# A hybrid decoder trunk on one Trainium2 core: the first layer's input projection in another order of column chunks

## The chip, the cores and the metric

The kernel runs on one core of a Trainium2 chip. The metric is the device time of one execution in microseconds (us), lower is better. A core has TensorE (PE, with its weight loads shown as PEld), VectorE (DVE), ScalarE (ACT), GpSimd (POOL) and SyncE (SP, which here issues nearly all plain DMAs), and 16 DMA engines that serve them.

## The reference

Two residual layers over 512 rows of 1024 float32 values. What matters here is the first half of layer 0:

```python
xn = rms_norm(x, mix_norm_even[i])
proj = jnp.einsum('bsd,de->bse', xn, w_in[i])
au, av, q, kc, vc, ks, vs, kw, vw, gl = jnp.split(proj, split_points, axis=-1)
ya = chunked_spatial_gating(au, av, ...)                  # gelu(au) * (W_s @ rms_norm(gelu(av)) + b_s)
yb = native_sparse_attention(q, kc, vc, ks, vs, kw, vw, gl, ...)
x = x + jnp.einsum('bse,ed->bsd', jnp.concatenate([ya, yb], axis=-1), w_out[i])
# inside the attention: 8 query heads, 2 kv heads, head size 64
q = rms_norm(q.reshape(bsz, seq, G, H, D), q_gain) * (HEAD_DIM ** -0.5)
k_cmp = rms_norm(compress(kc, w_cmp_k), k_gain[0]); v_cmp = compress(vc, w_cmp_v)
ks, kw = rms_norm(ks, k_gain[1]), rms_norm(kw, k_gain[2])
g = jax.nn.sigmoid(gate_logits)                           # weights of the three branches
```

The 2328 columns of `w_in` are: au 512, av 512, q 512, six tensors of 128 (kc, vc, ks, vs, kw, vw) and 24 gate logits. After this half comes a mixture of 32 experts (its weights are most of the bytes), and then layer 1: a pooling mixer and a second mixture of experts. All is float32.

## The kernel before

It is written engine by engine, each with its own instruction stream in program order; semaphores join them. The 512 rows are four blocks of 128 (`NB = 4`), the 1024 inputs are eight blocks (`KD = 8`).

**Projection.** `x_transpose(b)` transposes a row block on PE into banks 0 to 3, ACT and DVE copy it out with the norm's gain (`x_out`), and ACT and DVE make its root mean square (`square`, `mean`, `root`, `rroot`). The projection goes by column chunks, in the order of the list `CH`: q (512 columns), kc to vs (512), kw, vw and gates (280), a_v (512), a_u (512). `project(ch, b)` is one tile: eight products of 128 x 128 by 128 x n into bank 4 + i % 4, with i = 4 ch + b. From i = 4 on it waits until the tile four places back has been copied out (`s_pe_`). `proj_tile(ch, b)` is ACT's copy of that tile to SBUF, scaled by the row's 1/rms; a_v goes through Gelu and is squared there.

**Weights of the chunks.** There are two buffers, `win[0]` and `win[1]`; chunk ch goes to `win[ch % 2]`. SP issues, in its program order: the first row block of x, the first gain, chunk 0 (in two halves, L457), the other three row blocks, chunk 1, 14 small loads and the router's, the weights of the first expert pair (`load_gate_up(0, 0, ...)` L431, `load_down` L442), zeros for a DRAM buffer (L486), and only then chunk 2, when chunk 0 has been multiplied (`s_pj`, L422). Behind it come the four loads of the compression weights (L496), chunk 3 when chunk 1 is done, and chunk 4 when chunk 2 is done. All of these are on one hardware DMA queue.

```python
for ch in range(2, len(CH)):
    sp.wait_ge(s_pj, 4 * (ch - 1))
    load_win(ch)
```

**Head norms.** When all of the first three chunks are copied out, ACT squares q, ks and kw (L842, L844, L845), DVE sums them by head (L1146 to L1148), ACT takes the root (L847), DVE inverts it (L1153) and scales q in four instructions and the keys in eight (L1077 under `tt`). Behind that in DVE's program stand the inputs of the compression: copies of the transposed kc and vc (L1169) and additions into `cmp_in`. PE meanwhile transposes kc and vc (L1618), runs `project(3, 0)` and `project(3, 1)`, waits for the scaled q and keys (`s_qk_n` 6), transposes three blocks of q, and waits for `s_ci` before the 256 small products of the compression (L1652). `project(3, 2)`, more transposes, `project(3, 3)` and the a_u tiles (`gate_rows`, L1674) follow, these between the 32 attention units.

**Gates.** ACT makes exp(-rstd * logit) straight from the product's bank, from `minus_rstd` that DVE prepares (L1141).

Of the kernel before, what the change touches and what calls it, by code (L numbers as in the profile page):

```python
# [20 lines left out]
ALU = mybir.AluOpType  # L21
# [3 lines left out]
P = 128  # L25
# [20 lines left out]
def build(nc, t):  # L46
    ctx = ExitStack()
    with ctx:
# [3 lines left out]
        def sem(name):  # L52
            return ctx.enter_context(nc.semaphore(name))
# [48 lines left out]
        vrstd = mix[:, 528:544]  # L102
        minus_rstd = vrstd[:, 0:NB]
        gate = mix[:, 544:640]
# [17 lines left out]
        def bank(i):  # L122
# [63 lines left out]

        CH = [("q", 1024, 512), ("kc_vc_ks_vs", 1536, 512), ("kw_vw_gates", 2048, 280),
              ("a_v", 512, 512), ("a_u", 0, 512)]
# [12 lines left out]
        s_w = sems("win_loaded", len(CH))  # L201
        s_w0b = sem("first_win_second_half_loaded")
        s_gain = sem("first_gain_loaded")
# [198 lines left out]
        def _(sp):  # L402
# [50 lines left out]

            w_first = t["w_in"][0].rearrange("(p k) n -> p k n", k=KD)
            for h in range(2):
                ks = slice(4 * h, 4 * h + 4)
                sp.dma_start(win[0].rearrange("p (k n) -> p k n", k=KD)[:, ks, :],  # L457
                             w_first[:, ks, CH[0][1]:CH[0][1] + 512]).then_inc(s_w0b if h else s_w[0], 16)
            for b in range(1, NB):
# [288 lines left out]
        def _(act):  # L748
# [20 lines left out]
            def rows(n, b):  # L769
                act.wait_ge(s_rs, stat(n, b) + 1)  # L770
                if n == 3 and b < NB - 1:
                    act.wait_ge(s_pt2, b + 2)
                if n == 3:
                    act.wait_ge(s_pt2, b + 1)
                a.activation(xs[:, b, :], x3[:, b, :], ACT.Copy,
                             scale=rstd[:, n * NB + b:n * NB + b + 1]).then_inc(s_xs[b], 1)
# [39 lines left out]
            def proj_tile(ch, b):  # L816
                i = 4 * ch + b
                act.wait_ge(s_pj, i + 1)
                src = bank(4 + i % 4)
                own = rstd[:, b:b + 1]  # L820
                if ch == 0:
                    act.wait_ge(s_rs, stat(0, b))

                    a.activation(q[:, b, :].rearrange("p (i g d) -> p g i d", i=4, g=2),
                                 src.rearrange("p (g i d) -> p g i d", g=2, i=4), ACT.Copy, scale=own).then_inc(s_pe_, 1)
                elif ch == 1:
                    a.activation(kv[:, b, 0:512], src, ACT.Copy, scale=own).then_inc(s_pe_, 1)
                elif ch == 2:
                    act.wait_ge(s_rs, stat(0, NB - 1) + 1)
                    a.activation(kv[:, b, 512:768], src[:, 0:256], ACT.Copy, scale=own)  # L830
                    a.activation(gate[:, b * 24:(b + 1) * 24], src[:, 256:280], ACT.Exp,
                                 scale=minus_rstd[:, b:b + 1]).then_inc(s_pe_, 1)
                else:
                    a.activation(v[:, b, :], src, ACT.Gelu, scale=own).then_inc(s_pe_, 1)
                    act.wait_ge(s_pe_, i + 1)
                    a.activation(v_squares[:, b, :], v[:, b, :], ACT.Square).then_inc(s_vs, 1)

            for ch in range(3):
                for b in range(NB):
                    proj_tile(ch, b)  # L840
            act.wait_ge(s_pe_, 12)
            a.activation(squares.rearrange("p (b c) -> p b c", b=NB), q, ACT.Square).then_inc(s_hs, 1)  # L842
            sq2 = squares2.rearrange("p (r b c) -> p r b c", r=2, b=NB)
            a.activation(sq2[:, 0], kv[:, :, 256:384], ACT.Square).then_inc(s_hs, 1)  # L844
            a.activation(sq2[:, 1], kv[:, :, 512:640], ACT.Square).then_inc(s_hs, 1)  # L845
            act.wait_ge(s_mean, 1)
            a.activation(hstd[:, :], hsq[:, :], ACT.Sqrt).then_inc(s_std, 1)  # L847
            act.wait_ge(s_small, SMALL)
            link(a.activation(q_gain[:, :], q_gain[:, :], ACT.Copy, scale=HD ** -0.5))

            def q_out(i):
                act.wait_ge(s_mt, 3 + i)
                a.activation(qT[:, i, :], bank((0, 1, 3, 0)[i]), ACT.Copy, scale=q_gain[:, 0:1]).then_inc(s_mta, 1)
# [9 lines left out]
            proj_tile(3, 0)  # L863
            proj_tile(3, 1)
            act.wait_ge(s_cm, 1)
            q_out(0)
            q_out(1)
            q_out(2)
            act.wait_ge(s_mean, 2)
            a.activation(csq[0:HD, 1:2], csq[0:HD, 0:1], ACT.Sqrt).then_inc(s_std, 1)  # L870
            proj_tile(3, 2)
            q_out(3)
            k_out(0)
            k_out(1)
            proj_tile(3, 3)
            act.wait_ge(s_mean, 3)
            a.activation(vstd[:, :], vsq[:, :], ACT.Sqrt).then_inc(s_std, 1)
# [189 lines left out]
        def _(dve):  # L1067
# [71 lines left out]
            rroot(0, NB - 1)  # L1139
            dve.wait_ge(s_rs, stat(0, NB - 1))  # L1140
            ve.tensor_scalar(minus_rstd, rstd[:, 0:NB], -1.0, None, ALU.mult).then_inc(s_rs, 1)  # L1141
            dve.wait_ge(s_small, SMALL)


            dve.wait_ge(s_hs, 3)
            ve.tensor_reduce(hsq[:, 0:32], squares.rearrange("p (a d) -> p a d", d=HD), AX, ALU.add)  # L1146
            link(ve.tensor_reduce(hsq[:, 32:48], squares2.rearrange("p (a d) -> p a d", d=HD), AX, ALU.add))
            ve.tensor_scalar(hsq[:, :], hsq[:, :], 1.0 / HD, EPS, ALU.mult, ALU.add).then_inc(s_mean, 1)  # L1148

            link(ve.tensor_scalar(gate[:, :], gate[:, :], 1.0, None, ALU.add))  # L1150
            ve.reciprocal(gate[:, :], gate[:, :])
            dve.wait_ge(s_std, 1)
            link(ve.reciprocal(hrstd[:, :], hstd[:, :]))  # L1153
            qv = q.rearrange("p b (h d) -> p b h d", d=HD)
            hv = hrstd[:, 0:32].rearrange("p (b h) -> p b h", b=NB)
            for b in range(NB):
                tt(qv[:, b], qv[:, b], bc(hv[:, b], 2, [P, NH, HD]), ALU.mult).then_inc(s_qk_n, 1)
            for r in range(2):
                c0 = 256 + 256 * r
# [5 lines left out]

            dve.wait_ge(s_cz, 2)
            for r in range(2):
                dve.wait_ge(s_mt, 1 + r)
                link(ve.tensor_copy(rawT[:, r, :], bank(r)))  # L1169
                dve.sem_inc(s_mtv, 1)  # L1170
                for half in range(2):
# [15 lines left out]
            v_sum(0)  # L1187
            v_sum(1)

# [10 lines left out]
            ins.then_inc(s_vb, 1)  # L1200
            dve.wait_ge(s_std, 2)
            link(ve.reciprocal(csq[0:HD, 2:3], csq[0:HD, 1:2]))
            link(ve.tensor_scalar(kcn[0:HD, 0:HD], kcn[0:HD, 0:HD], csq[0:HD, 2:3], None, ALU.mult))
            link(tt(kcn[0:HD, 0:HD], kcn[0:HD, 0:HD], kc_gain[0:HD, :], ALU.mult))
            ve.tensor_copy(kcn[0:HD, HD:2 * HD], kcn[0:HD, 0:HD]).then_inc(s_kn, 1)
            v_sum(2)
            dve.wait_ge(s_kt, 1)
# [80 lines left out]
            maxes(1)  # L1288
            dve.wait_ge(s_std, 3)
            ve.reciprocal(vrstd[:, :], vstd[:, :]).then_inc(s_vn, 1)  # L1290
# [47 lines left out]
            def route(l):  # L1338
                lgt = rt["lgt"].rearrange("p (b c) -> p b c", b=NB)
                n = 1 + 2 * l  # L1340
                dve.wait_ge(s_lg, NB * (l + 1))
                dve.wait_ge(s_rs, stat(n, NB - 1) + 1)
                link(tt(lgt, bank(LOGIT_BANK[l])[:, 0:144].rearrange("p (b c) -> p b c", b=NB),
# [211 lines left out]
        def _(pe_):  # L1555
# [41 lines left out]
            def project(ch, b):  # L1597
# [10 lines left out]
                for k in range(KD):  # L1608
                    if i == 0 and k == 4:
                        pe_.wait_ge(s_w0b, 16)  # L1610
                    ins = mm(bank(4 + i % 4)[:, 0:n], xT[:, k, b * P:(b + 1) * P], w[:, k, :],  # L1611
                             start=(k == 0), stop=(k == KD - 1))
# [16 lines left out]
            for ch in range(1, 3):  # L1629
                for b in range(NB):  # L1630
                    project(ch, b)

            pe_.wait_ge(s_pe_, 8)
            transpose_blocks(bank(0), kv, 0)
            transpose_blocks(bank(1), kv, P)
            project(3, 0)
            project(3, 1)
            pe_.wait_ge(s_qk_n, 6)
            pe_.wait_ge(s_mtv, 1)
            transpose_blocks(bank(0), q, 0)  # L1640
            pe_.wait_ge(s_mtv, 2)
            transpose_blocks(bank(1), q, P)
            transpose_blocks(bank(3), q, 2 * P)

# [420 lines left out]
```

## Time and profile before

| | before |
|---|---|
| Median of 3 runs | 896.33 us (894.91, 896.59, 896.33) |
| The profiled execution's own time | 892.19 us |
| Its span in the trace | 890.4 us |
| PE busy | 791.5 us, 89% of the span |
| ACT, DVE busy | 242.6 us, 255.4 us |
| Projection, chunks 0 to 2, in the trace | 9.9 to 85.3 us |
| Chunk 3 with compression and transposes | 85.3 to 124.9 us |
| First attention units on | from 128.5 us |

The span is what the hardware profiler recorded between the first and last instruction; the profiled execution's own time has 1.8 us around it. A timeline line gives start, duration, engine, line of the program, and in square brackets the idle time before it and who ended it. "DMA to landing" counts from the start of the issuing instruction on SP to the moment the data are announced.

### The profile page before, as it was taken

The page shows a single profiled execution, that of the slowest core. Times are in us where ns is not written, and L with a number is a line of the kernel's source. Part 1 is how long each engine was busy: PE and PEld are TensorE (multiplying, and loading weights), DVE is VectorE, ACT ScalarE, POOL GpSimd, SP SyncE. Part 2 cuts the span into 40 slices and gives each one's busy share as a digit, 9 for nine tenths or more (in the row PEclk, how much of TensorE's full clock was granted, in tenths as well). Part 3 has the DMA queues.
Part 4 walks back from the last instruction along what each step waited for, and adds up shares of the span by engine and source line. Part 5 has one row for each costly group of instructions (what it writes and reads, how often), then busy time and mean ns, then how long its engine had stood idle before and what let it go on. Part 6 is the DMA issues. An engine that isn't in the chain of part 4 may idle for free.

```text
span 890.4 us, 10328 instructions
## 1 busy us (share of the span) xinstructions
PE 791.5 (89%) x3981; PEld 375.3 (42%) x3981; DVE 255.4 (29%) x577; ACT 242.6 (27%) x584; POOL 100.1 (11%) x164
## 2 busy tenths in 40 slices
PE   6999899999999989998877978899999996797965
PEld 3447444555555633333322322397433332332321
DVE  0100727566462351111101111554511111111106
ACT  3303355554344411221101111364012211111111
POOL 2000000000002510111101001130111111011000
PEclk9999999999999999999988999999999999888998
DMA  8898130200002599999999999996399999999986
GB/s 287 259 328 189 64 78 18 95 2 1 0 1 79 205 404 406 416 357 421 421 421 419 419 415 391 386 421 252 141 392 418 419 419 423 420 420 418 406 312 253
DMA packets 74912, 258.09 MB, mean 290 GB/s; under 512 B 28017, under 2 KB 29553, under 8 KB 54896
## 3 DMA queue, kind: packets, MB, share of 16 engines
q1 hardware_dynamic: 65936, 241.16, 69.2%
q0 software_dynamic: 8928, 16.27, 4.9%
q8 instruction: 32, 0.52, 0.2%
q14 instruction: 16, 0.13, 0.0%
HBM read 247.44 MB, written 26.21 MB: 307 GB/s over the span
## 4 chain that ended last, share of the span: by engine, by line
PE 71%; DMA 10%; DVE 8%; issue 4%; ACT 3%; SPq 3%; DVEq 1%; POOLq 0%
PE ps L1884 22%; PE ps L1898 10%; PE ps L1611 10%; PE ps L1762 6%; DMA rest<-in_w_exp_down_dram 5%; PE ps L1878 3%; PE ps L1674 3%; PE ps L1818 2%; PE ps L1573 2%; PE ps L1686 2%; PE ps L1830 2%; SPq L442 2%; DMA norm<-expert_rows 2%; PE ps L2013 2%; PE ps L1591 2%
## 5 line engine op out<-in xcount | busy, mean ns | idle before, releaser
L1884 PE MATMUL ps<-w_pair,tmp 128*64 128x512 f32 x704 | 172.1, 644 | 38.1 <-issue 17.7
L1884 PEld LDWEIGHTS ps<-w_pair,tmp 128*64 128x64 f32 x704 | 55.8, 148 | 140.2 <-issue 124.9
L1611 PE MATMUL ps<-w_pair,norm 128*128 128x512 f32 (+1 forms) x256 | 100.5, 552 | 4.2 <-DMA w_pair<-in_w_in_dram 3.7
L1077 DVE TENSOR_TENSOR tmp<-tmp,ps 128x256 f32<-128x256 f32 (+1 forms) x34 | 13.8, 407 | 294.7 <-ACT tmp L962 294.7
L962 ACT ACTIVATE tmp<-ps 128x256 f32<-128x256 f32 x32 | 12.3, 384 | 272.4 <-PE ps L1884 272.4
L1898 PE MATMUL ps<-w_pair,tmp 128*64 128x512 f32 x352 | 80.4, 598 | 3.2 <-ACT tmp L965 2.0
L1884 PE MATMUL ps<-norm,tmp 128*64 128x512 f32 x320 | 72.8, 607 | 10.5 <-issue 7.3
L1611 PEld LDWEIGHTS ps<-w_pair,norm 128*128 128x128 f32 x256 | 48.8, 193 | 52.3 <-issue 45.2
L657 POOL DMA_INDIRECT expert_rows<-tmp x30 | 30.2, 1005 | 331.1 <-DVE tmp L1467 314.2
L1762 PE MATMUL ps<-w_pair,norm 128*128 128x512 f32 x128 | 58.0, 593 | 0.0
L957 ACT ACTIVATE tmp<-ps,gains 128x128 f32<-128x128 f32 x128 | 36.6, 369 | 61.1 <-PE ps L1878 61.1
L1467 DVE COPY tmp<-ps 128x512 f32<-128x512 f32 x30 | 20.8, 692 | 93.3 <-PE ps L1898 93.3
L651 POOL DMA_INDIRECT tmp<-norm_rows,tmp x32 | 32.8, 1026 | 119.2 <-DVEq L1424 57.6
L1884 PEld LDWEIGHTS ps<-norm,tmp 128*64 128x64 f32 x320 | 23.6, 139 | 52.5 <-issue 47.2
L1878 PEld LDWEIGHTS ps<-ident,tmp 128*128 128x128 f32 x256 | 31.1, 194 | 32.3 <-issue 29.5
L1573 PE MATMUL ps<-masks 128*128 128x512 bf16 x186 | 44.7, 400 | 0.0
L1878 PE MATMUL ps<-ident,tmp 128*128 128x128 f32 x256 | 36.8, 287 | 7.4 <-issue 6.9
L1898 PEld LDWEIGHTS ps<-w_pair,tmp 128*64 128x64 f32 x352 | 23.7, 136 | 43.5 <-issue 38.8
L973 ACT ACTIVATE tmp<-ps 128x512 f32<-128x512 f32 x30 | 17.9, 598 | 82.6 <-PE ps L1898 82.6
L921 ACT ACTIVATE rest<-ps 128x768 f32<-128x768 f32 (+3 forms) x32 | 21.6, 677 | 64.0 <-PE ps L1818 64.0
L1898 PE MATMUL ps<-rest,tmp 128*64 128x512 f32 x160 | 36.5, 597 | 2.5 <-DMA rest<-in_w_exp_down_dram 2.5
L889 ACT ACTIVATE rest<-ps,mix_small 128x384 f32<-128x384 f32 (+3 forms) x64 | 32.3, 511 | 3.4 <-DVE mix_small L1271 3.1
(241 smaller groups left out, 832.7 us busy)
## 6 DMA issues: line engine op xcount, KB each, us to landing
w_pair<-in_w_exp_gate_dram SPq DMA_DIRECT2D x44, 1024.0 KB, 17.6
w_pair<-in_w_exp_up_dram SPq DMA_DIRECT2D x44, 1024.0 KB, 26.1
w_pair<-in_w_exp_down_dram SPq DMA_DIRECT2D x40, 1024.0 KB, 26.9
rest<-in_w_exp_down_dram SPq DMA_DIRECT2D x20, 1024.0 KB, 22.1
norm<-in_w_exp_gate_dram SPq DMA_DIRECT2D x20, 1024.0 KB, 23.1
norm<-in_w_exp_up_dram SPq DMA_DIRECT2D x20, 1024.0 KB, 27.6
norm<-expert_rows SPq DMA_DIRECT2D x16, 512.0 KB, 8.3
w_pair<-in_w_in_dram SPq DMA_DIRECT2D x3, 2048.0 KB, 10.1
```

What stands on the lines that cost most here:

```text
L651: return pool.indirect_dma_start(out=buf, out_offset=None, in_=norm_dram, in_offset=bass.IndirectOffsetOnAxis(ap=index, axis=0), bounds_ch ...
L657: return pool.indirect_dma_start(out=out_dram, out_offset=bass.IndirectOffsetOnAxis(ap=index, axis=0), in_=buf, in_offset=None, bounds_che ...
L889: ins = a.activation(prob[:, n % 2, h, 0:width], bank(2 * (n % 2) + h)[:, 0:width], ACT.Exp, bias=nmax[:, 2 * n + h:2 * n + h + 1], accum_ ...
L921: a.activation(pT[:, n % 2, 0:nb], ps[2][:, :, :].rearrange("p c n -> p (c n)")[:, 0:256 * nb] .rearrange("p (a h t) -> p a h t", h=2, t=P ...
L957: ins = a.activation(xgT[:, k, :], bank(0)[:, k * P:(k + 1) * P], ACT.Copy, scale=gain_v[:, n, k:k + 1])
L1573: mm(o, identb, masks[:, 0:512], start=True, stop=True)
L1611: ins = mm(bank(4 + i % 4)[:, 0:n], xT[:, k, b * P:(b + 1) * P], w[:, k, :], start=(k == 0), stop=(k == KD - 1))
L1674: ins = mm(bank(7), xT[:, k, b * P:(b + 1) * P], w[:, k, :], start=(k == 0), stop=(k == KD - 1))
L1762: ins = mm(out_bank(b, half), xT[:, k, b * P:(b + 1) * P], wout[:, k, half * 512:(half + 1) * 512], start=(j == 0), stop=(j == KD - 1))
L1878: ins = te.transpose(bank(k // 4)[:, (k % 4) * P:(k % 4 + 1) * P], xv[:, k, :], ident[:, :])
L1884: ins = mm(bank(2)[64 * a:64 * a + 64, :], xgT[:, k, 64 * a:64 * a + 64], gu[w][:, a, :, k * FE:(k + 1) * FE], start=(k == 0), stop=(k == ...
L1898: ins = mm(bank(4 + half)[64 * a:64 * a + 64, :], hidT[:, jj, 64 * a:64 * a + 64], dn[w][:, a, c0:c0 + 512], start=(jj == 0), stop=(jj == 1))
```

## The change

The order of the chunks becomes kw, vw and gates (280 columns); q; kc to vs; a_v; a_u. Chunk 0 is loaded in one piece. Eight products of the identity with itself stand on PE between the first transposes and the first tile. ACT copies the gate logits and takes the exponential of all at once; squares of kw are taken after chunk 0, those of q after chunk 1, and the roots of both after the first tile of chunk 2; only ks is left for after chunk 2. DVE's program is reordered the same way: it scales q and kw first, then prepares the compression's inputs, then scales ks. PE transposes the third block of q ahead of kc and vc, one tile of chunk 3 stands ahead of the compression instead of two, and the second a_v sum on DVE comes later. `minus_rstd` and its wait go.

```diff
-        CH = [("q", 1024, 512), ("kc_vc_ks_vs", 1536, 512), ("kw_vw_gates", 2048, 280),
+        CH = [("kw_vw_gates", 2048, 280), ("q", 1024, 512), ("kc_vc_ks_vs", 1536, 512),
               ("a_v", 512, 512), ("a_u", 0, 512)]
...
-            w_first = t["w_in"][0].rearrange("(p k) n -> p k n", k=KD)
-            for h in range(2):
-                ks = slice(4 * h, 4 * h + 4)
-                sp.dma_start(win[0].rearrange("p (k n) -> p k n", k=KD)[:, ks, :],
-                             w_first[:, ks, CH[0][1]:CH[0][1] + 512]).then_inc(s_w0b if h else s_w[0], 16)
+            load_win(0)
...
-            for ch in range(3):
-                for b in range(NB):
-                    proj_tile(ch, b)
+            sq2 = squares2.rearrange("p (r b c) -> p r b c", r=2, b=NB)
+            for b in range(NB):
+                proj_tile(0, b)
+            act.wait_ge(s_pe_, 4)
+            a.activation(gate[:, :], gate[:, :], ACT.Exp, scale=-1.0)
+            a.activation(sq2[:, 1], kv[:, :, 512:640], ACT.Square).then_inc(s_hs, 1)
+            for b in range(NB):
+                proj_tile(1, b)
+            act.wait_ge(s_pe_, 8)
+            a.activation(squares.rearrange("p (b c) -> p b c", b=NB), q, ACT.Square).then_inc(s_hs, 1)
+            proj_tile(2, 0)
+            act.wait_ge(s_mean, 1)
+            a.activation(hstd[:, 0:32], hsq[:, 0:32], ACT.Sqrt)
+            a.activation(hstd[:, 40:48], hsq[:, 40:48], ACT.Sqrt).then_inc(s_std, 1)
+            for b in range(1, NB):
+                proj_tile(2, b)
             act.wait_ge(s_pe_, 12)
-            a.activation(squares.rearrange("p (b c) -> p b c", b=NB), q, ACT.Square).then_inc(s_hs, 1)
-            sq2 = squares2.rearrange("p (r b c) -> p r b c", r=2, b=NB)
             a.activation(sq2[:, 0], kv[:, :, 256:384], ACT.Square).then_inc(s_hs, 1)
-            a.activation(sq2[:, 1], kv[:, :, 512:640], ACT.Square).then_inc(s_hs, 1)
-            act.wait_ge(s_mean, 1)
-            a.activation(hstd[:, :], hsq[:, :], ACT.Sqrt).then_inc(s_std, 1)
+            act.wait_ge(s_mean, 2)
+            a.activation(hstd[:, 32:40], hsq[:, 32:40], ACT.Sqrt).then_inc(s_std, 1)
...
+            k_scaled(1)
+
+            dve.wait_ge(s_hs, 3)
+            link(ve.tensor_reduce(hsq[:, 32:40], sq2[:, 0], AX, ALU.add))
+            head_mean(slice(32, 40)).then_inc(s_mean, 1)
+            dve.wait_ge(s_cz, 2)
+            cmp_input(0)
+            cmp_input(1)
+            dve.wait_ge(s_std, 2)
+            link(ve.reciprocal(hrstd[:, 32:40], hstd[:, 32:40]))
+            k_scaled(0)
...
             x_transpose(0)
+            for _ in range(8):
+                mm(bank(7)[:, 0:P], ident[:, :], ident[:, :], start=True, stop=True)
             project(0, 0)
...
-            pe_.wait_ge(s_pe_, 8)
+            pe_.wait_ge(s_qk_n, 4)
+            transpose_blocks(bank(3), q, 2 * P)
+            pe_.wait_ge(s_pe_, 12)
             transpose_blocks(bank(0), kv, 0)
             transpose_blocks(bank(1), kv, P)
             project(3, 0)
-            project(3, 1)
-            pe_.wait_ge(s_qk_n, 6)
             pe_.wait_ge(s_mtv, 1)
             transpose_blocks(bank(0), q, 0)
             pe_.wait_ge(s_mtv, 2)
             transpose_blocks(bank(1), q, P)
-            transpose_blocks(bank(3), q, 2 * P)
```

## Rows read from the trace of the kernel before

**Rows 1.** The page: PE's busy share in 40 slices of the span, in tenths.
```profile
PE   6999899999999989998877978899999996797965
```

**Rows 2.** PE's timeline, 0 to 125 us; in brackets idle time before and its releaser.
```profile
9.90 8.90 PE L1611 MATMUL ps<-w_pair,norm 128*128 128x512 f32 x16 [3.73 <-DMA w_pair<-in_w_in_dram]
...
101.42 1.09 PE L1618 MATMUL ps<-ident,rest 128*128 128x128 f32 x8 [1.09 <-DVEq L1170]
103.51 2.98 PE L1652 MATMUL ps<-norm,tmp 64*32 64x64 f32 x197 [0.99 <-DVE tmp L1077]
...
124.85 3.67 PE L1674 MATMUL ps<-w_pair,norm 128*128 128x512 f32 x8 [0.67 <-ACT tmp L834]
```

**Rows 3.** The chain that ended last, 60 to 125 us: start, us, what.
```profile
59.90 25.41 PE ps L1611 x88
...
101.46 1.91 DVE tmp L1077 x2
...
106.49 1.16 issue
...
108.73 7.06 PE ps L1611 x16
115.80 1.31 PE ps L1618 x12
```

**Rows 4.** SP's timeline: when the DMAs of the start were issued (queue instructions).
```profile
30.20 0.51 SPq L431 DMA_DIRECT2D w_pair<-in_w_exp_gate_dram  x1
...
35.33 0.45 SPq L486 DMA_DIRECT2D expert_rows<-tmp  x1
42.76 0.56 SPq L422 DMA_DIRECT2D w_pair<-in_w_in_dram  x1
```

**Rows 5.** DMA sizes by line, first 90 us: times issued, KB each, us to landing.
```profile
w_pair<-in_w_exp_gate_dram SPq DMA_DIRECT2D x2, 1024.0 KB
w_pair<-in_w_exp_down_dram SPq DMA_DIRECT2D x2, 1024.0 KB, 16.4
expert_rows<-tmp SPq DMA_DIRECT2D x1, 4096.0 KB, 26.5
w_pair<-in_w_in_dram SPq DMA_DIRECT2D x1, 1120.0 KB, 22.4
```

**Rows 6.** Landing of the last x block (L413), then chunk 3's load (L422).
```profile
DMA to landing us min/median/max: 11.8/12.0/12.2
DMA to landing us min/median/max: 10.1/10.1/10.1
```

**Rows 7.** By stretch: PE, PEld, DVE, ACT, POOL busy (x), granted clock, DMA share, GB/s.
```profile
2.00:8.00 6.00, 1.95 (x8) 1.57 (x8) 0.69 (x1) 1.73 (x3) 4.46 (x23) 1.00 0.91 289
8.00:18.00 10.00, 8.10 (x15) 3.61 (x16) 0.32 (x2) 3.22 (x7) 0.20 (x2) 1.00 1.04 398
48.00:60.00 12.00, 12.00 (x29) 5.32 (x28) 0.00 (x0) 1.37 (x2) 0.00 (x0) 1.00 1.02 409
```

**Rows 8.** ACT's timeline: copies of tiles, with ACT's idle time before each.
```profile
70.23 0.69 ACT L827 ACTIVATE w_pair<-ps,rstd 128x512 f32<-128x512 f32 x1 [6.18 <-PE ps L1611]
...
81.56 0.47 ACT L830 ACTIVATE w_pair<-ps,rstd 128x256 f32<-128x256 f32 x1 [3.12 <-PE ps L1611]
...
85.33 0.47 ACT L830 ACTIVATE w_pair<-ps,rstd 128x256 f32<-128x256 f32 x1 [3.13 <-PE ps L1611]
```

**Rows 9.** PE matmuls in 9.8 to 11 and in 16 to 18.8 us: xcount, busy, mean ns.
```profile
L1611 PE MATMUL ps<-w_pair,norm 128*128 128x512 f32 x2 | 2.1, 1142 | 3.7 <-DMA w_pair<-in_w_in_dram 3.7
...
L1611 PE MATMUL ps<-w_pair,norm 128*128 128x512 f32 x7 | 3.2, 592 | 0.0
```

**Rows 10.** PE's timeline in the expert stages: tiles after an idle time.
```profile
435.06 7.09 PE L1884 MATMUL ps<-norm,tmp 128*64 128x512 f32 x32 [2.75 <-issue]
...
451.84 9.74 PE L1884 MATMUL ps<-w_pair,tmp 128*64 128x512 f32 x32 [4.59 <-issue]
...
518.99 8.60 PE L1884 MATMUL ps<-w_pair,tmp 128*64 128x512 f32 x32 [5.16 <-DMA w_pair<-in_w_exp_up_dram]
```

More of the change, by code:

```diff
@@ L102, in build @@
         vrstd = mix[:, 528:544]
-        minus_rstd = vrstd[:, 0:NB]
         gate = mix[:, 544:640]
@@ L201, in build @@
         s_w = sems("win_loaded", len(CH))
-        s_w0b = sem("first_win_second_half_loaded")
         s_gain = sem("first_gain_loaded")
@@ L769, in rows @@
             def rows(n, b):
-                act.wait_ge(s_rs, stat(n, b) + 1)
+                act.wait_ge(s_rs, stat(n, b))
                 if n == 3 and b < NB - 1:
@@ L822, in proj_tile @@
                     act.wait_ge(s_rs, stat(0, b))
+                    a.activation(kv[:, b, 512:768], src[:, 0:256], ACT.Copy, scale=own)
+                    a.activation(gate[:, b * 24:(b + 1) * 24], src[:, 256:280], ACT.Copy, scale=own).then_inc(s_pe_, 1)
+                elif ch == 1:
                     a.activation(q[:, b, :].rearrange("p (i g d) -> p g i d", i=4, g=2),
                                  src.rearrange("p (g i d) -> p g i d", g=2, i=4), ACT.Copy, scale=own).then_inc(s_pe_, 1)
-                elif ch == 1:
+                elif ch == 2:
                     a.activation(kv[:, b, 0:512], src, ACT.Copy, scale=own).then_inc(s_pe_, 1)
[L828 to L832, printed above, removed]
                 else:
@@ L851, in q_out @@
             def q_out(i):
-                act.wait_ge(s_mt, 3 + i)
+                act.wait_ge(s_mt, (4, 5, 1, 6)[i])
                 a.activation(qT[:, i, :], bank((0, 1, 3, 0)[i]), ACT.Copy, scale=q_gain[:, 0:1]).then_inc(s_mta, 1)
@@ L863, in _ @@
             proj_tile(3, 0)
-            proj_tile(3, 1)
             act.wait_ge(s_cm, 1)
@@ L868, in _ @@
             q_out(2)
-            act.wait_ge(s_mean, 2)
+            act.wait_ge(s_mean, 3)
             a.activation(csq[0:HD, 1:2], csq[0:HD, 0:1], ACT.Sqrt).then_inc(s_std, 1)
-            proj_tile(3, 2)
+            proj_tile(3, 1)
             q_out(3)
@@ L874, in _ @@
             k_out(1)
+            proj_tile(3, 2)
             proj_tile(3, 3)
-            act.wait_ge(s_mean, 3)
+            act.wait_ge(s_mean, 4)
             a.activation(vstd[:, :], vsq[:, :], ACT.Sqrt).then_inc(s_std, 1)
@@ L1139, in _, with head_mean, k_scaled @@
             rroot(0, NB - 1)
-            dve.wait_ge(s_rs, stat(0, NB - 1))
-            ve.tensor_scalar(minus_rstd, rstd[:, 0:NB], -1.0, None, ALU.mult).then_inc(s_rs, 1)
             dve.wait_ge(s_small, SMALL)
[L1145 to L1158, printed above, removed]
+            sq2 = squares2.rearrange("p (r a d) -> p r a d", r=2, d=HD)
+            def head_mean(c):
+                return ve.tensor_scalar(hsq[:, c], hsq[:, c], 1.0 / HD, EPS, ALU.mult, ALU.add)
+            def k_scaled(r):
                 c0 = 256 + 256 * r
@@ L1164, in _, with cmp_input @@
                 ins.then_inc(s_qk_n, 1)
-            dve.wait_ge(s_cz, 2)
-            for r in range(2):
-                dve.wait_ge(s_mt, 1 + r)
+            def cmp_input(r):
+                dve.wait_ge(s_mt, 2 + r)
                 link(ve.tensor_copy(rawT[:, r, :], bank(r)))
@@ L1176, in _ @@
                 ins.then_inc(s_ci, 1)
+            dve.wait_ge(s_hs, 1)
+            ve.tensor_reduce(hsq[:, 40:48], sq2[:, 1], AX, ALU.add)
+            dve.wait_ge(s_hs, 2)
+            link(ve.tensor_reduce(hsq[:, 0:32], squares.rearrange("p (a d) -> p a d", d=HD), AX, ALU.add))
+            head_mean(slice(0, 32))
+            head_mean(slice(40, 48)).then_inc(s_mean, 1)
+            link(ve.tensor_scalar(gate[:, :], gate[:, :], 1.0, None, ALU.add))
+            ve.reciprocal(gate[:, :], gate[:, :])
+            dve.wait_ge(s_std, 1)
+            ve.reciprocal(hrstd[:, 0:32], hstd[:, 0:32])
+            link(ve.reciprocal(hrstd[:, 40:48], hstd[:, 40:48]))
+            qv = q.rearrange("p b (h d) -> p b h d", d=HD)
+            hv = hrstd[:, 0:32].rearrange("p (b h) -> p b h", b=NB)
+            for b in range(NB):
+                tt(qv[:, b], qv[:, b], bc(hv[:, b], 2, [P, NH, HD]), ALU.mult).then_inc(s_qk_n, 1)
+            k_scaled(1)
[8 more added lines that the diff above has]
+            k_scaled(0)
             def v_sum(b):
@@ L1187, in _ @@
             v_sum(0)
-            v_sum(1)
             dve.wait_ge(s_cm, 1)
@@ L1200, in _ @@
             ins.then_inc(s_vb, 1)
-            dve.wait_ge(s_std, 2)
+            dve.wait_ge(s_std, 3)
             link(ve.reciprocal(csq[0:HD, 2:3], csq[0:HD, 1:2]))
@@ L1205, in _ @@
             ve.tensor_copy(kcn[0:HD, HD:2 * HD], kcn[0:HD, 0:HD]).then_inc(s_kn, 1)
+            v_sum(1)
             v_sum(2)
@@ L1288, in _ @@
             maxes(1)
-            dve.wait_ge(s_std, 3)
+            dve.wait_ge(s_std, 4)
             ve.reciprocal(vrstd[:, :], vstd[:, :]).then_inc(s_vn, 1)
@@ L1341, in route @@
                 dve.wait_ge(s_lg, NB * (l + 1))
-                dve.wait_ge(s_rs, stat(n, NB - 1) + 1)
+                dve.wait_ge(s_rs, stat(n, NB - 1))
                 link(tt(lgt, bank(LOGIT_BANK[l])[:, 0:144].rearrange("p (b c) -> p b c", b=NB),
@@ L1608, in project @@
                 for k in range(KD):
-                    if i == 0 and k == 4:
-                        pe_.wait_ge(s_w0b, 16)
                     ins = mm(bank(4 + i % 4)[:, 0:n], xT[:, k, b * P:(b + 1) * P], w[:, k, :],
@@ L1654, in _ @@
             ins.then_inc(s_cm, 1)
-            project(3, 2)
+            project(3, 1)
             pe_.wait_ge(s_mta, 1)
             transpose_blocks(bank(0), q, 3 * P)
+            pe_.wait_ge(s_qk_n, 6)
             pe_.wait_ge(s_mta, 2)
@@ L1661, in _ @@
             transpose_blocks(bank(3), kv, 512)
+            project(3, 2)
             project(3, 3)
```

## The prediction

> **What bounds the kernel now.** First the page: PE's digits are 8 or 9 in most slices [rows 1], so the change is worth what it takes out of PE's stream or puts into it. Then PE's timeline over the stretch that it touches, from 9.90 us, where the first tile starts after 3.73 us of waiting for its weights, to 124.85, where the a_u tiles start. Behind chunk 0 there are four short gaps: 1.09 us until DVE frees a bank, 0.99 us until the compression's inputs are ready [rows 2], 1.16 us that the chain calls issue [rows 3], and 0.67 us at the end [rows 2]. Chunks 1 and 2 are one unbroken run. A 512-column tile takes 6.87 us and a 280-column tile 3.77 us, as ACT's copies show, which follow each tile at once (6.18 idle and 0.69 busy; 81.56 to 85.33) [rows 8]. Last the DMA side. SP issues the first expert pair and the zeros from 30.20 to 35.33 us, and only at 42.76 the load of chunk 2, today the narrow one [rows 4]. It lands 22.4 us later [rows 5], at 65.2, and PE wants it at 70.2, when chunk 1 ends [rows 8]. That margin of 5.0 us is the number to watch: the change puts a full chunk there and wants it sooner.
>
> **When chunk 2 is wanted.** From 9.90 to 42.76 (the end of chunk 0, for which SP's load waits [rows 4]) PE spends 32.9 us: four tiles of 6.87 are 27.5, the other 5.4 are transposes, a gap and a slow first tile (8.90 us for 6.87, so 2.0 [rows 2, 8]). With the narrow chunk first the tiles are 15.1 us, and chunk 0 ends at 9.9 + 15.1 + 5.4 = 30.4, or 28.4 if the eight products save the slow tile. Chunk 1 (q) adds 27.5: it ends at 55.9 to 57.9. PE's wish moves from 70.2 to about 57.
>
> **When chunk 2 is there.** Its load still stands behind the first expert pair and the zeros: two gate, two up and two down loads of 1024 KB and 4096 KB of zeros [rows 5], together 10240 KB, 10.5 MB. The zeros land at 35.33 + 26.5 = 61.8 us, and the narrow chunk (1120 KB, 1.15 MB), issued 7.4 us behind them, 3.3 us after them [rows 4, 5]. That is its bytes at the 409 GB/s of this stretch [rows 7], 2.8 us, and 0.5 us. So the queue serves in order, and waiting for chunk 0 costs this load nothing today; issuing it earlier buys nothing. In the changed kernel it has 2048 KB (2.10 MB): 5.1 + 0.5 = 5.6 us after the zeros, 67.4. Something comes back at the front. Chunk 0's load is smaller by 0.95 MB, 2.4 us at 398 GB/s or 3.3 us at 289 [rows 7]. It moves the expert loads forward as far as SP is held by a full queue in the first stretch; the last x block lands 12.2 us after its issue [rows 6], so the queue is deep then, and I take 2.4 us. Chunk 2 lands at **65.0 us**; bounds 67.4 if nothing comes back, 63.6 if 3.3 us do and the 0.5 go.
>
> **The end of chunk 2.** PE waits from about 57 to 65.0, some 8 us. Everything that the change saves or costs before is inside this wait: the eight products (at most the 3.7 us for which PE waits today), the first tile's speed, one DMA in place of two halves. Then four tiles, 27.5 us. Tiles behind an idle time are slow: 32 matmuls take 7.09 us behind 2.75 us idle, but 8.60 behind 5.16 and 9.74 behind 4.59 [rows 10]. So 0 to 2.65 us are lost; I take 1.7, between the row with the longest idle time (1.5) and the first tile's 2.0. Chunk 2 ends at 65.0 + 27.5 + 1.7 = 94.2 us, before at 85.3 [rows 3]: **8.9 us later**.
>
> Here a page and a row part. The granted clock reads 1.00, which is 2.4 GHz, for 8 to 18 us [rows 7], though the first matmuls take 1142 ns and the later ones 592 [rows 9]. The Trainium skill, "TensorE: Matmul & The Clock Gate", section "The HAM clock gate (the 'warmup' mystery)", says that the default state is throttled, that activity releases the throttle, and that the clock events of a trace have been seen to be unreliable. By the granted clock alone the wait would cost no speed, and the forecast would be 1.7 us lower; by the page it costs what the durations show.
>
> **From there to the a_u tiles.** Today 85.3 to 124.85, 39.5 us. In the new order PE transposes q's third block, 0.4 us. Q is scaled by then: its squares, sums, roots and products on ACT and DVE lie beside the wait and chunk 2. PE then waits for ACT's copy of the last tile, 0.7 us from the chunk's end, so 0.3 new. Eight transposes 0.9, a tile 6.9. Beside that tile DVE makes the ks sum and both compression inputs. Today an input's two additions take 1.91 us [rows 3]; with its copy and the steps between, an estimate of 2.7, 5.4 for both. With 2.2 us for ACT's copy, squares and the ks sum ahead they are ready at about 7.7, and PE wants them at 9.4: the gaps of 1.09 and 0.99 go. Then transposes 0.9, the compression 5.2 with its 1.16 of issue (103.51 to 108.73 [rows 2, 3]), a tile 7.1, twelve transposes 1.3 [rows 3], two tiles 13.8, and a last gap of 0.8, for ACT copies the last tile either way. Sum 0.4 + 0.3 + 0.9 + 6.9 + 0.9 + 5.2 + 7.1 + 1.3 + 13.8 + 0.8 = 37.6: **1.9 us gained**. Bounds: nothing, if DVE is as late as now; 3.1, if the issue gap goes too.
>
> **Parts at nothing.** The gates' copies and one exponential for four, the split roots with a table load, and `minus_rstd` lie on ACT and DVE under tiles of 3.8 to 6.9 us, with four banks between; ACT idles 6.18 us before a copy [rows 8]. Without that cover they would cost some 2 us. The root that ACT waits for behind chunk 2's first tile holds its next copy, and so PE only four tiles on. On SP's queue the four compression loads and chunk 3's load stand behind the bigger chunk. Chunk 3's load goes out at 70.23 today, when chunk 1 ends [rows 8], and lands 10.1 us later [rows 6], at 80.3; even 3 us more is early for 96. Chunk 4's load waits for chunk 2's end and is used 40 us behind it. POOL's pads wait for a mean that comes earlier.
>
> **On to the end.** Behind 125 us nothing goes by absolute time: the first expert pair is there, and the next loads wait for the attention's last products. I take the difference as passed on in full: 8.9 - 1.9 = **+7.0 us**. On the profiled execution that is 892.19 + 7.0 = 899.2 (its span would be 897.4). The median of the runs is 4.1 us above that execution; for it the forecast is 896.33 + 7.0 = **903.3 us**.
>
> **Rivals.**
> 1. Faster: chunk 2 is there in time, because a late load doesn't wait for those queued before it. Then it ends at 55.9 + 27.5 = 83.4, 1.9 us before now, and with the 1.9 behind it the kernel gains 3.8: 892.5. It decides at the landing: at 59.7 the kernel is even (59.7 + 27.5 - 1.9 = 85.3). By 65.2 the queue has brought 11.6 MB from 30.2 us on, 333 GB/s with the landing's lag; for 59.7 it would have to bring 12.6 MB from 27.8 on, 395 GB/s. The order of the landings speaks against it. 0.12.
> 2. The landing at 63.6 and no slow tile: 7.0 - 1.4 - 1.7 = +3.9, 900.2. The cold rows speak against it, the row behind 2.75 us for it. 0.20.
> 3. The same with the issue gap gone and the queue faster still, within 1.8 us of now. 0.08.
> 4. The norms stay late, the change not doing what it says, and SP gets nothing back: 7.0 + 1.9 + 2.4 = +11.3, 907.6. DVE's list is shorter by the q and kw work, which speaks against the first. 0.16.
> 5. The forecast, +5 to +9: 0.44.
>
> **How the numbers follow.** The likeliest case gives 903.3. The range goes from 897.8, where case 2 thins out, to 908.0, just past case 4; outside lie rival 1, case 3 and the tails, 2 in 10. The runs of before spread over 1.7 us; 0.2%, 1.8 us, is about what a measurement of this kernel can tell from no change. Faster 0.12, within 0.2% 0.08, slower 0.80.
>
> **What would show it.** In the changed profile: the loop's first load (L422) issued right behind the zeros at 33 to 36 us; PE idle 6 to 10 us near 57 with the load of w_in as releaser, and a slow tile behind it; chunk 2's last copy on ACT at 92 to 97; no gap at q's transposes nor before the compression; the a_u tiles from about 132. The prediction is wrong if that idle time is missing (rival 1), or if the a_u tiles start 7 us late and the end does not.

## The result, and the profile after

| | before | changed |
|---|---|---|
| Median of 5 runs | 894.91 us (891.49 to 896.59) | 903.61 us (900.47 to 905.99) |
| Ratio | | 1.0089, 95% interval 1.0064 to 1.0114 |
| Profiled execution, own time | 892.19 us | 900.47 us |
| Its span | 890.4 us | 898.3 us |
| Last copy of chunk 2 begins | 85.33 us | 94.95 us |
| a_u tiles begin | 124.85 us | 132.77 us |

The changed kernel is slower by 8 us, 0.9%. Its PE timeline, 0 to 140 us (start, us, engine, line, operation, in brackets the idle time before and its releaser), answers to [rows 2]:

```profile
5.96 2.76 PE L1640 MATMUL ps<-ident 128*128 128x128 f32 x16
8.83 4.01 PE L1628 MATMUL ps<-w_pair,norm 128*128 128x280 f32 x16
...
28.99 27.70 PE L1628 MATMUL ps<-w_pair,norm 128*128 128x512 f32 x64 [1.49 <-ACT mix_small L818]
65.32 29.59 PE L1628 MATMUL ps<-w_pair,norm 128*128 128x512 f32 x64 [8.63 <-DMA w_pair<-in_w_in_dram]
94.75 0.60 PE L1635 MATMUL ps<-ident,rest 128*128 128x128 f32 x4
95.69 1.09 PE L1635 MATMUL ps<-ident,w_pair 128*128 128x128 f32 x8 [0.34 <-ACT w_pair L824]
96.62 7.03 PE L1628 MATMUL ps<-w_pair,norm 128*128 128x512 f32 x16
103.49 1.04 PE L1635 MATMUL ps<-ident,rest 128*128 128x128 f32 x8
104.46 2.99 PE L1669 MATMUL ps<-norm,tmp 64*32 64x64 f32 x198
...
132.77 3.67 PE L1693 MATMUL ps<-w_pair,norm 128*128 128x512 f32 x8 [0.67 <-ACT tmp L826]
```

The first part worked: the first tile runs at full speed behind the eight products (4.01 us, as the second), and chunk 1 ends at 56.7 us. Then PE stands for 8.63 us, and the bracket names the load of w_in. The four tiles behind the wait take 29.6 us where chunk 1's took 27.7. The gaps of 1.09 and 0.99 us at q's transposes and ahead of the compression are gone; 0.34 us are new. SP's timeline of the changed kernel, beside [rows 4]:

```profile
28.36 0.51 SPq L429 DMA_DIRECT2D w_pair<-in_w_exp_gate_dram  x1
...
32.68 0.48 SPq L480 DMA_DIRECT2D expert_rows<-tmp  x1
33.20 10.26 SPq L420 DMA_DIRECT2D w_pair<-in_w_in_dram  x1
```

Chunk 2's load is issued right behind the zeros, 9.6 us sooner than before, and here is its landing (the answer for that one issue, from the start of the instruction):

```profile
DMA to landing us min/median/max: 32.1/32.1/32.1
```

33.2 + 32.1 = 65.3 us: issued 9.6 us earlier, landed 0.1 us later than the narrow chunk before [rows 4, 5]. The issue itself took 10.26 us on SP, for 0.56 before [rows 4]; I read that as a full queue, which no run tests.

The rest of the kernel moved as a block: from the a_u tiles to the end of the span there are 765.5 us before and 765.5 after. That the two agree so well is luck: in the profiled executions of the experiments below the same stretch, in which the edits change no work, takes 765.6 to 770.9 us.

### The profile page after: what moved, and what is told of

Same layout as the page of the kernel before. It is cut to its first block, busy times and chain, and to the rows that moved or that the text cites. A ratio compares the mean times of both kernels' runs of the same rounds, so it can differ in the third digit from the quotient of the medians.

```text
span 898.3 us, 10362 instructions
## 1 busy us (share of the span) xinstructions
PE 793.7 (88%) x3997; PEld 377.2 (42%) x3997; DVE 256.0 (28%) x581; ACT 242.8 (27%) x587; POOL 99.8 (11%) x164
## 4 chain that ended last, share of the span: by engine, by line
PE 65%; DMA 13%; SPq 8%; DVE 6%; issue 4%; ACT 3%; DVEq 0%; POOLq 0%; ACTq 0%
PE ps L1903 20%; PE ps L1917 9%; PE ps L1628 7%; PE ps L1781 6%; DMA rest<-in_w_exp_down_dram 5%; DMA w_pair<-in_w_in_dram 4%; SPq L433 3%; PE ps L1897 3%; PE ps L1693 3%; SPq L440 2%; PE ps L1837 2%; PE ps L1592 2%; PE ps L1705 2%; PE ps L1849 2%; DMA norm<-expert_rows 2%
```

## Experiments

Each ran beside the kernel before on the same chip. Two numbers are read from each: the ratio of times with its interval, and the start of the a_u tiles in the profiled execution, which leaves out the scatter of the later stages.

### Chunk 2's load ahead of the expert loads

```diff
+            sp.wait_ge(s_pj, 4)
+            load_win(2)
             load_gate_up(0, 0, 0)
...
             for ch in range(2, len(CH)):
-                sp.wait_ge(s_pj, 4 * (ch - 1))
-                load_win(ch)
+                if ch > 2:
+                    sp.wait_ge(s_pj, 4 * (ch - 1))
+                    load_win(ch)
```

> The changed kernel with one edit: SP issues the load of chunk 2 ahead of the first expert pair and the zeros (still waiting for chunk 0 to be multiplied). Theory (the 8.6 us wait is the place in the queue): the load is issued at about 28 us, lands by 35, PE runs from chunk 1 (ends at 56.7) straight into chunk 2, which ends at 84.2; the a_u tiles start at 84.2 + 37.8 = 122.0, 10.8 us before the changed kernel's 132.8 and 2.9 before the kernel before's 124.85. Median about 892. Rival 1 (the DMA engines are simply short of time, so that the next load in line is late instead: compression weights or chunk 3): a new wait of some us at chunk 3 or before the compression, median 897 to 901. Rival 2 (the wait is inherent in a full chunk on this place): no change, 903.

Measured: median 893.46 us beside 896.10, ratio 0.9981 (0.9958 to 1.0004). PE's timeline of this kernel, from chunk 0's last tiles on:

```profile
20.39 62.78 PE L1631 MATMUL ps<-w_pair,norm 128*128 128x280 f32 x160
83.01 0.60 PE L1638 MATMUL ps<-ident,rest 128*128 128x128 f32 x4
...
121.01 3.67 PE L1696 MATMUL ps<-w_pair,norm 128*128 128x512 f32 x8 [0.67 <-ACT tmp L829]
```

Ten tiles in one run of 62.78 us without a gap, and the a_u tiles 11.8 us before the changed kernel's. The load of chunk 2 landed at 37.8 us (issued at 28.14, 9.7 to landing). The theory's 122.0 was 1 us too late. ACT still waited for the small loads, but they landed 1.0 us sooner in this execution (27.2 for 28.2 us), and PE came to the fifth tile 0.6 us later, so PE's own wait of 1.49 us did not arise. Rival 1, that another load becomes late, is out for this chunk order, rival 2 too. The change's own work is worth 3.8 us of PE's time once the load is in place. The interval of the ratio just reaches 1, though, and by itself doesn't prove a gain over the kernel before.

### Half of the zeros behind chunk 2's load

```diff
-            sp.dma_start(out_dram.rearrange("(r p) d -> p r d", p=P), zeros.unsqueeze(1).to_broadcast([P, 8, D]))\
-              .then_inc(s_zst, 16)
+            zero_rows = out_dram.rearrange("(r p) d -> p r d", p=P)
+            for h in range(2):
+                if h:
+                    sp.wait_ge(s_pj, 4)
+                    load_win(2)
+                sp.dma_start(zero_rows[:, 4 * h:4 * h + 4, :], zeros.unsqueeze(1).to_broadcast([P, 4, D]))\
+                  .then_inc(s_zst, 16)
...
-            pool.wait_ge(s_zst, 16)
+            pool.wait_ge(s_zst, 32)
```

The loop over the chunks behind it skips chunk 2, as in the first experiment.

> The changed kernel with the zeros' DMA in two halves and chunk 2's load between them: 2.1 MB less ahead of it than in the changed kernel, all else in place. Theory (in order, by bytes): it lands 2.1 MB / 409 GB/s = 5.1 us earlier, at 60.2; PE idles 3.5 us instead of 8.6; a_u tiles at about 127.7, or up to 2 us less if the first tile is no longer slow; median about 898. If the queue were not served in order, its landing would stay near 65.

Measured: ratio 0.9994 (0.9969 to 1.0019), median 895.71. PE's timeline:

```profile
59.76 30.56 PE L1634 MATMUL ps<-w_pair,norm 128*128 128x512 f32 x64 [3.19 <-DMA w_pair<-in_w_in_dram]
...
128.20 3.67 PE L1699 MATMUL ps<-w_pair,norm 128*128 128x512 f32 x8 [0.67 <-ACT tmp L832]
```

2.1 MB less ahead of the load brought it 5.6 us forward (5.1 expected), and the wait from 8.63 to 3.19 us. That is the queue served in order, in a dose: with nothing moved PE waits 8.63 us, with 2.1 MB moved 3.19, with all of it moved not at all. The a_u tiles came only 4.6 us earlier, since the four tiles behind the shorter wait lost 2.9 us instead of 1.9 (30.56 and 29.59 against the 27.70 of chunk 1). The median is 2 us better than expected while the profiled execution, at 901.26 the slowest of its ten, is worse (its stretch behind the a_u tiles took 770.9 us); with this scatter I rest on the timeline.

### The changed kernel without the eight products

```diff
-            for _ in range(8):
-                mm(bank(7)[:, 0:P], ident[:, :], ident[:, :], start=True, stop=True)
```

> The changed kernel without the eight products ahead of the first tile. Theory: the first tile is slow again (about 2 us more), but chunk 0's end is covered twice, by the wait for the small loads (1.49 us on PE) and by the 8.6 us wait for chunk 2. The a_u tiles start at 132.8 as before, the time is the changed kernel's within 0.1%. Rival (the products matter by themselves, keeping PE fast): +2 us.

Measured: ratio to the kernel before 1.0119 (1.0077 to 1.0160), median 904.68. In PE's timeline the first tile is slow, PE's wait of 1.49 us for ACT is gone, and the wait for chunk 2 is 1.5 us shorter:

```profile
8.90 6.52 PE L1628 MATMUL ps<-w_pair,norm 128*128 128x280 f32 x16 [2.70 <-DMA w_pair<-in_w_in_dram]
...
64.70 29.64 PE L1628 MATMUL ps<-w_pair,norm 128*128 128x512 f32 x64 [7.15 <-DMA w_pair<-in_w_in_dram]
...
132.25 3.67 PE L1691 MATMUL ps<-w_pair,norm 128*128 128x512 f32 x8 [0.67 <-ACT tmp L826]
```

The first tile takes 6.52 us for 4.01. Of these 2.5 us the vanished wait for ACT takes 1.5, chunk 1 ends 0.9 us later, at 57.55, and the load of chunk 2, which landed 0.6 us sooner here, still comes long after that. The a_u tiles start at 132.25, not later than with the products: inside the wait they are worth nothing. The ratios, 1.0119 here and 1.0089 with the products, have intervals that overlap, so they show no difference.

### The same with the load in place

The two edits together: the load ahead, no products.

> Chunk 2's load ahead of the expert loads and the zeros, and no eight products. In the run with the products PE had no wait behind the first tile (chunk 0 ended at 28.1 us, chunk 2 at 83.0, a_u tiles at 121.0). Theory: the products are worth something only where no later wait covers them. The first tile is slow again, 6.5 us for 4.0, and now nothing hides it: a_u tiles at about 123.4, 2.4 us later than with them, unless the small loads end later than 28 us anyway; median 2 us above that run's. Rival (the wait for the small loads covers it): 121 to 121.5.

Measured: a_u tiles at 123.14 us, against 121.01 with the products, so 2.1 us.

```profile
8.88 6.79 PE L1631 MATMUL ps<-w_pair,norm 128*128 128x280 f32 x16 [2.67 <-ACT norm L797]
...
123.14 3.67 PE L1694 MATMUL ps<-w_pair,norm 128*128 128x512 f32 x8 [0.67 <-ACT tmp L829]
```

Here the loss of the slow first tile shows, as nothing behind it waits. The medians can't tell the two apart (893.48 here, ratio 0.9979, 0.9961 to 0.9997).

### The wait filled with work

```diff
             for ch in range(1, 3):
+                if ch == 2:
+                    pe_.wait_ge(s_const, 2)
+                    keep_warm(26, bank(3))
                 for b in range(NB):
                     project(ch, b)
```

> The changed kernel with 26 products of constants on PE (into a bank that nothing uses then) ahead of chunk 2, inside the 8.6 us wait. Theory (the tiles behind the wait are slow because PE stood idle): the landing stays at 65.3, the first 64 matmul records behind it take 27.7 us instead of 29.6, and the a_u tiles start at 130.8 instead of 132.8; median 2 us below the changed kernel. Rival (the slowness is something else, DMA traffic to SBUF or the weights' first read): 29.6 and 132.8.

The 26 products are bf16, of 512 columns each. Measured: median 902.52, ratio 1.0071 (1.0050 to 1.0093). PE's timeline:

```profile
55.95 5.56 PE L1592 MATMUL ps<-masks 128*128 128x512 bf16 x25
63.47 27.73 PE L1628 MATMUL ps<-w_pair,norm 128*128 128x512 f32 x64 [1.96 <-DMA w_pair<-in_w_in_dram]
...
129.06 3.67 PE L1696 MATMUL ps<-w_pair,norm 128*128 128x512 f32 x8 [0.66 <-ACT tmp L826]
```

The same 64 records take 27.73 us, as those of chunk 1. So the loss of the tiles behind the wait is what PE's standing idle costs; the traffic and the weights are the same in both. The landing was not at 65.3 as expected but at 63.4: in this execution SP issued the zeros at 31.06 us, not 32.68. Of the 3.7 us by which the a_u tiles come sooner, half is this landing (65.32 to 63.47) and half the speed (29.59 to 27.73).

### The load's place in the kernel before

The edit of the first experiment on the kernel before, alone.

> The kernel before with the same edit alone: chunk 2's load (narrow there) ahead of the first expert pair and the zeros. Theory (the place in the queue matters only where PE wants the load sooner than it lands): the load goes out at 42.8 and lands by 50, wanted at 70.2; the expert pair and the zeros now go out behind it, from 43 us, and the compression weights and chunk 3 behind those. No wait of PE is removed: a_u tiles at 124.9, the time of the kernel before. What could go against it: chunk 3's load, wanted at 86, then stands behind 10.5 MB that start 12.5 us later, and lands at 80 to 92; if it is late, PE waits up to 6 us there.

Measured: median 901.70, ratio 1.0070 (1.0043 to 1.0097). PE's timeline:

```profile
90.19 16.82 PE L1614 MATMUL ps<-w_pair,norm 128*128 128x512 f32 x32 [3.83 <-DMA w_pair<-in_w_in_dram]
...
129.50 3.67 PE L1677 MATMUL ps<-w_pair,norm 128*128 128x512 f32 x8 [0.66 <-ACT tmp L837]
```

The theory's first half missed, its exception came true: SP waited for chunk 0 until 42.95 us, the expert loads, the zeros and the compression weights followed, and chunk 3's load was issued at 78.9 instead of 70.2, with PE waiting for it until 90.2. The wait made the two tiles behind it slow too, 16.82 us for 13.90. So the edit is no gain in itself. With the full chunk first it blocks SP for 15 us longer than with the narrow one first (42.95 against 28.14 us).

### The order of the norms alone

The kernel before, with its chunks and loads, and with q's squares, roots and scaling during chunk 1, the new order on DVE, q's third block first, one tile of chunk 3 ahead of the compression:

```diff
+            for b in range(NB):
+                proj_tile(0, b)
+            act.wait_ge(s_pe_, 4)
+            a.activation(squares.rearrange("p (b c) -> p b c", b=NB), q, ACT.Square).then_inc(s_hs, 1)
+            proj_tile(1, 0)
+            act.wait_ge(s_mean, 1)
+            a.activation(hstd[:, 0:32], hsq[:, 0:32], ACT.Sqrt).then_inc(s_std, 1)
...
+            a.activation(gate[:, :], gate[:, :], ACT.Exp, scale=-1.0)
             a.activation(sq2[:, 0], kv[:, :, 256:384], ACT.Square).then_inc(s_hs, 1)
             a.activation(sq2[:, 1], kv[:, :, 512:640], ACT.Square).then_inc(s_hs, 1)
```

> One part alone: the kernel before, with its chunk order, its loads and no products, but q's squares, sums, roots and products during chunk 1, the compression's inputs ahead of the keys' scaling on DVE, q's third block transposed first and one tile of chunk 3 ahead of the compression. The keys' norms stay behind chunk 2. Theory: chunk 2 ends at 85.3 as before and the tail to the a_u tiles is 37.5 us instead of 39.5, so they start at 122.8 to 123; median 2 us below the kernel before. Rival (the norms' order is worth nothing, or the chunk order is needed for it): 124.85 and no difference.

Measured: no difference, ratio 1.0008 (0.9989 to 1.0027), a_u tiles at 124.87. The first tile took 10.03 us for 8.90 in the kernel before, so chunk 2 ended 0.8 us later; from there to the a_u tiles it was 38.7 us (86.18 to 124.87), 0.8 less than before, where 2 were expected. One gap had gone, the other not:

```profile
96.41 3.21 PE L1667 MATMUL ps<-norm,tmp 64*32 64x64 f32 x214 [1.22 <-DVE tmp L1081]
```

ACT's timeline of this kernel shows why:

```profile
86.85 1.28 ACT L847 ACT_TABLE_LOAD   x1
88.14 0.28 ACT L847 ACTIVATE mix_small<-mix_small 128x96 f32<-128x96 f32 x1
88.33 0.61 ACT L848 ACTIVATE rest<-w_pair 128x512 f32<-128x512 f32 x1
```

I had put the gates' exponential, and its table load, ahead of the keys' squares, and DVE's whole list waits for those. The next run moved it behind them:

```diff
-            a.activation(gate[:, :], gate[:, :], ACT.Exp, scale=-1.0)
             a.activation(sq2[:, 0], kv[:, :, 256:384], ACT.Square).then_inc(s_hs, 1)
             a.activation(sq2[:, 1], kv[:, :, 512:640], ACT.Square).then_inc(s_hs, 1)
+            a.activation(gate[:, :], gate[:, :], ACT.Exp, scale=-1.0).then_inc(s_hs, 1)
```

> The kernel before with the norms' order alone, as in the run of that name, but the gates' exponential (and its table load of 1.28 us) behind the squares of the keys instead of ahead of them. In that run the gap before q's transposes went, but the one before the compression stayed, 1.22 us, and the stretch from the last tile of chunk 2 to the a_u tiles was 38.7 us, not 37.5. Theory: the squares were late by the exponential and its table; now DVE starts 1.5 us earlier, the gap goes, the stretch is 37.5 us. Rival: DVE's two sums alone keep the inputs late, 38 to 38.7 us.

Measured: median 892.75 beside 896.36, ratio 0.9962 (0.9945 to 0.9980). ACT's last copy of chunk 2 begins here:

```profile
86.17 0.47 ACT L827 ACTIVATE w_pair<-ps,rstd 128x256 f32<-128x256 f32 x1 [3.13 <-PE ps L1629]
```

From it to the a_u tiles, at 123.43, there are 37.3 us, before 39.5. The gap is gone, and the a_u tiles start 1.4 us earlier than in the kernel before in spite of a first tile of 10.12 us. The norms' order is worth 2 us of the path and doesn't need the chunk order, if no table load stands ahead of the squares.

### Two versions put together

> The kernel before with the norms' order alone (exponential behind the squares) and the eight products ahead of the first tile; chunk order and loads as before. In the run without the products the first tile took 10.1 us, chunk 2 ended at 86 and the a_u tiles started at 123.4. Theory: with them the first tile takes 7.1 us, nothing behind it waits for the small loads (chunk 0 ends at 40), so the a_u tiles start 2.5 to 3 us earlier, at 120.5 to 121, and the median is 4 us (3 to 5.5) below the kernel before. Rival (the products run past the landing of the weights and cost what they give): 123.

Measured (the last kernel and the eight products): first tile 7.05 us, ratio 0.9956 (0.9929 to 0.9982), median 893.35.

```profile
120.39 3.67 PE L1694 MATMUL ps<-w_pair,norm 128*128 128x512 f32 x8 [0.67 <-ACT tmp L830]
```

In the timeline the products give 3.0 us (123.43 to 120.39), as the theory has it. The times don't show them: without the products the ratio was 0.9962, 0.9945 to 0.9980.

```diff
-            act.wait_ge(s_small, SMALL)
...
             def proj_tile(ch, b):
```

> The changed kernel with chunk 2's load ahead of the expert loads, and ACT's first wait for all small loads gone (they are waited for once more behind chunk 2, where they are used). Theory: PE's wait for ACT's copies ahead of chunk 1 (1.49 us in the changed kernel, 0 in the first run with the load ahead) can no longer arise, everything else stays: a_u tiles at 121.0, median as in that run, 2.5 to 4 us below the kernel before. Rival (that wait was of use, by holding ACT's copies off something): later than 121.5.

Measured (the first experiment's kernel and this edit on ACT): ratio 0.9968 (0.9946 to 0.9989), median 891.43.

```profile
120.64 3.67 PE L1695 MATMUL ps<-w_pair,norm 128*128 128x512 f32 x8 [0.67 <-ACT tmp L828]
```

Both versions are faster than the kernel before, by 0.1 to 0.7%, and can't be told apart. What made the a_u tiles of this one start 0.4 us earlier than its base's is the start of the first tile (9.00 against 9.52), not the small loads, for which PE did not wait in its base's execution either. Whether the edit on ACT is worth anything is open.

## Why the prediction was right, point by point

- **The place in the queue.** Predicted: the load issued at 33 to 36 us, landed at 65.0; measured 33.2 and 65.3. Two errors cancelled. The zeros landed at 32.68 + 26.1 = 58.8, 3.0 us sooner than before, where I had taken 2.4; but the full chunk came 6.5 us behind them, not 5.6. The dose of the half zeros (5.6 us for 2.1 MB) and the kernel with the load ahead show that the place in the queue is the cause.
- **When the chunk is wanted.** 55.9 to 57.9 predicted, 56.7 measured. It held although I had missed two things that nearly cancelled: chunk 0's smaller load landed at 8.6 us, not 9.9, and PE waited 1.49 us for ACT, which was waiting for the small loads. The prediction doesn't name this wait; what covers it is its sentence that everything before is inside the wait for chunk 2.
- **Speed behind the wait.** 1.7 us predicted, 1.9 measured (29.59 us for chunk 1's 27.70); filling the wait removes it. Chunk 2's last copy starts 29.6 us behind the landing, 0.4 later than the 27.5 + 1.7 of the sum: 0.2 of it is this loss, and 0.2 the lag from the first product to the copy, which chunk 1 has too (28.99 to 56.73) and the sum left out. The granted clock does show the loss. By stretch (PE, PEld, DVE, ACT, POOL busy, granted clock, DMA share, GB/s):

```profile
57.00:65.00 8.00, 0.00 (x0) 0.00 (x0) 3.41 (x5) 2.33 (x2) 0.21 (x2) 0.62 1.09 296
65.00:95.00 30.00, 29.68 (x67) 13.21 (x68) 3.72 (x10) 3.72 (x7) 0.00 (x0) 0.93 0.54 125
```

  Taken apart, the second stretch has its low clock at the start:

```profile
65.32:69.00 3.68, 3.68 (x5) 1.61 (x6) 0.00 (x0) 0.00 (x0) 0.00 (x0) 0.50 1.16 201
69.00:70.00 1.00, 1.00 (x4) 0.52 (x3) 0.00 (x0) 0.00 (x0) 0.00 (x0) 0.95 1.34 215
70.00:95.00 25.00, 25.00 (x62) 11.08 (x61) 3.72 (x10) 3.72 (x7) 0.00 (x0) 1.00 0.42 111
```

  A clock of 0.50, which is 1.2 GHz, for 3.8 us is a loss of 1.9 us. In the filled kernel the stretch has 1.00:

```profile
63.00:91.00 28.00, 27.53 (x64) 12.24 (x65) 3.72 (x10) 3.67 (x6) 0.00 (x0) 1.00 0.61 139
```

  So of the two readings in the prediction the one with the loss held. The Trainium skill says it too ("TensorE: Matmul & The Clock Gate", section "The HAM clock gate (the 'warmup' mystery)"): the default state is throttled, and activity releases the throttle. The trace agrees, with 0.50 behind the idle time and 1.00 from 70 us on. The 1.00 that I had set against it [rows 7] is from the very start, where the first tiles are slow and the record shows nothing; in mid-kernel record and durations agree.
- **From chunk 2's end to the a_u tiles.** 37.6 predicted, 37.8 measured (94.95 to 132.77). The norms' order alone gives 37.3.
- **Parts at nothing.** The eight products, the gates' copies and the split roots cost nothing in the changed kernel. For the products that is shown by the runs with and without the wait. Chunk 3's load, issued at 69.7, landed at 81.2, long before PE wanted it at 96.6.
- **Passing on.** +7.9 us at the a_u tiles, +7.9 in the span, +8.3 in the profiled executions' times. Nothing was given back, as far as a stretch that by itself varies by 5 us can show it.
- **The rivals.** The first, chunk 2 there in time, is refuted by the wait. The second, a landing at 63.6 and no slow tile, missed in both halves: 65.3 and 1.9 us. The third needed the issue gap gone and the queue faster still: the gap stayed, at 1.27 us. The fourth falls with the missing gaps, and for SP with the expert loads, which it issued 1.8 us sooner than before (28.36 against 30.20).

The sum of +7.0 stands against +7.9 in the spans and 8.0 by the ratio, and that the median of 903.61 us came within 0.3 of the forecast is partly luck. The forecast was built on 896.33 us from three runs; with two more the median of before is 894.91, and over 23 to 29 runs in the experiments it is 896.10 to 896.81. The spread of 1.7 us that the prediction took from those three runs was far too small: 29 runs of the kernel before lie between 890.93 and 899.38.

## What to carry to other kernels

When steps are reordered so that a wide operand comes where a narrow one was, follow the load and not the product: on a queue served in order the bytes ahead of it set its landing, and issuing it 9.6 us sooner behind the same bytes did not bring it sooner. A prefetch for a later stage belongs behind the loads that the next stages want, as far as the issuing engine need not wait for a buffer first; the same edit brought the a_u tiles 11.8 us forward where that wait ended at 28 us and put them 4.7 us back where it ended at 43. Work that shortens a stage shows its worth only when no wait behind it covers it, so try it once more with the wait gone.

## What the runs showed of the hardware

- A shorter wait cost more speed than a long one: behind 8.63 and 7.15 us idle four tiles lost 1.9 us, behind 3.19 us 2.9, and two tiles behind 3.83 us 2.9 too; behind 1.96 us nothing was lost. The tiles of [rows 10] are of the same kind, 2.65 us lost behind 4.59 us and 1.5 behind 5.16. The granted clock shows where the difference lies. It fell to 0.50 between 2.1 and 4.2 us after PE had stopped, and it came back 3.8 us after PE had begun again in the changed kernel, but 5.7 us after in the kernels with half of the zeros behind and with the load's place changed alone:

```profile
59.76:65.00 5.24, 5.24 (x6) 2.18 (x7) 2.91 (x5) 0.00 (x0) 0.21 (x2) 0.50 0.91 249
65.00:66.00 1.00, 1.00 (x3) 0.53 (x2) 0.00 (x0) 0.00 (x0) 0.00 (x0) 0.76 0.62 144
```

```profile
90.19:95.00 4.81, 4.81 (x6) 2.19 (x7) 4.71 (x8) 0.59 (x3) 0.21 (x2) 0.50 0.99 364
95.00:96.00 1.00, 1.00 (x2) 0.34 (x1) 1.00 (x3) 0.00 (x0) 0.00 (x0) 0.55 0.00 0
```

  Half of 3.8 and of 5.7 us are the losses measured. What decides how long the clock stays low no run varied, so that is open.
- The executions of one kernel scatter by 5 to 10 us where ten or more were timed: those of the kernel with the load ahead lie between 889 and 898 us, those of the norms' order with the products between 887 and 897. Their profiled executions start the a_u tiles at 121.01 and 120.39 and have spans of 886.7 and 891.2. The mean granted clock differs in the same sense, 0.969 and 0.961; over 400 to 500 us it is 0.91 in the first and 0.93 in the second, over 700 to 800 us 0.93 and 0.91. Why it differs stays open. For effects under 4 us the start of a stage in the trace told more than the twelve timed runs.
